# Decode attention started twelve dense units earlier, as one chain of FoX key steps in which VectorE turns K

## What is computed

```python
proj = einsum('bsd,de->bse', h, w_in)                 # q_f k_f v_f f_logit q_d k_d v_d
gates = sigmoid(einsum('bsd,de->bse', h, w_gate) + b_gate)
# FoX, 8 heads, 16 pages of 128 past tokens per sample, taken through page_table
s = einsum('bqhd,bshd->bhqs', q, k) * SCALE + bias_q + bias_k   # bias_k: suffix sum of the cached log forget gates
o_fox = einsum('bhqs,bshd->bqhd', softmax(where(causal, s, NEG)), v)
# dilated windows, 3 groups x 4 heads, keys by stride, T5 bias, merged by their softmax denominators
y = (g_fox * (o_fox @ w_o_fox) + g_dil * (o_dil @ w_o_dil)) @ w_out
```

## Time and profile before

| | us |
|---|---|
| runs, median of 3 | 2433.61 |
| lowest and highest run | 2426.76, 2433.73 |
| the profiled execution | 2423.86 |
| its span | 2422.2 |

### The profile page before, as it was taken

How to read it: one execution, slowest core, us unless ns; L and a number is a source line. 1 busy time by engine, 2 the same in 40 slices (tenths; PEclk the granted TensorE clock), 3 DMA queues, 4 the chain that set the end, 5 groups by cost and what they waited for, 6 DMA issues and landing times.

```text
span 2422.2 us, 45416 instructions
## 1 busy us (share of the span) xinstructions
PE 2330.6 (96%) x18348; PEld 2131.0 (88%) x18348; DVE 1063.4 (44%) x1446; ACT 811.0 (33%) x986; POOL 465.9 (19%) x876
## 2 busy tenths in 40 slices
PE   6999999998999899989989998999999999999998
PEld 6999999998766667666659997999999999999998
DVE  6443434433333333333327437544444444444444
ACT  3233233232433333333412334323333232323334
POOL 2120000002233233323321230311111111111110
PEclk8999999999999999999999999999999999999999
DMA  8474535436899999999976644767677767688894
GB/s 251 141 218 154 155 120 163 152 113 203 279 361 363 340 339 360 362 330 352 343 264 209 217 139 146 267 232 250 228 233 238 245 224 239 222 286 267 288 308 131
DMA packets 337905, 589.57 MB, mean 243 GB/s; under 512 B 17503, under 2 KB 279971, under 8 KB 334079
## 3 DMA queue, kind: packets, MB, share of 16 engines
q0 software_dynamic: 68112, 312.68, 36.7%
q1 hardware_dynamic: 269648, 274.86, 35.8%
HBM read 564.06 MB, written 113.06 MB: 280 GB/s over the span
## 4 chain that ended last, share of the span: by engine, by line
PE 83%; DMA 10%; issue 2%; DVE 2%; ACT 1%; POOL 1%; SPq 0%; POOLq 0%; DVEq 0%; ACTq 0%
PE ps L838 15%; PE ps L839 15%; PE ps L840 15%; PE ps L876 6%; PE ps L878 6%; PE ps L877 6%; DMA kraw<-in_cache_win_k 4%; DMA kraw<-in_cache_fox_k 3%; PE ps L1066 3%; PE ps L1071 2%; PE ps L1091 2%; PE ps L1151 2%; PE ps L1055 2%; PE ps L1057 1%; PE ps L1056 1%
## 5 line engine op out<-in xcount | busy, mean ns | idle before, releaser
L1692 DVE TENSOR_TENSOR w_lo<-raw,w_hi 128x2048 fp32r<-128x2048 f32 (+2 forms) x248 | 526.6, 2124 | 762.3 <-ACT w_hi L1359 762.3
L1359 ACT ACTIVATE w_hi<-raw 128x2048 fp32r<-128x2048 f32 (+2 forms) x248 | 435.6, 1756 | 1032.6 <-PE ps L840 732.6
L838 PE MATMUL ps<-act_hi,w_hi 128*128 128x320 f32 x1616 | 499.6, 309 | 2.0 <-DVE w_lo L1692 2.0
L840 PE MATMUL ps<-act_hi,w_lo 128*128 128x320 f32 x1616 | 499.3, 309 | 0.0
L839 PE MATMUL ps<-act_lo,w_hi 128*128 128x320 f32 x1616 | 499.3, 309 | 0.0
L876 PE MATMUL ps<-act_hi,w_hi 128*128 128x320 f32 x1008 | 318.2, 316 | 0.0
L878 PE MATMUL ps<-act_hi,w_lo 128*128 128x320 f32 x1008 | 312.2, 310 | 0.0
L877 PE MATMUL ps<-act_lo,w_hi 128*128 128x320 f32 x1008 | 312.0, 310 | 0.0
L838 PEld LDWEIGHTS ps<-act_hi,w_hi 128*128 128x128 f32 x1616 | 303.3, 188 | 2.5 <-DVE w_lo L1692 2.5
L839 PEld LDWEIGHTS ps<-act_lo,w_hi 128*128 128x128 f32 x1616 | 303.3, 188 | 0.0
L840 PEld LDWEIGHTS ps<-act_hi,w_lo 128*128 128x128 f32 x1616 | 303.3, 188 | 0.0
(11 more groups left out here) (381 smaller groups left out, 3756.6 us busy)
## 6 DMA issues: line engine op xcount, KB each, us to landing
raw<-in_w_gate_up SPq DMA_DIRECT2D x88, 1024.0 KB, 7.5
kraw<-in_cache_fox_k POOLq DMA_DIRECT2D x128, 512.0 KB, 6.5
vraw<-in_cache_fox_v POOLq DMA_DIRECT2D x128, 512.0 KB, 6.9
raw<-in_w_in SPq DMA_DIRECT2D x60, 1024.0 KB, 7.8
raw<-in_w_down SPq DMA_DIRECT2D x32, 1024.0 KB, 6.0
out_win_k_sample<-in_cache_win_k POOLq DMA_DIRECT2D x64, 510.0 KB, 6.0
out_win_v_sample<-in_cache_win_v POOLq DMA_DIRECT2D x64, 510.0 KB, 4.2
raw<-in_w_gate SPq DMA_DIRECT2D x52, 512.0 KB, 11.0
```

Of the source, the lines that this page charges most:

```text
L838: pe.matmul(ps[:, bk_, 0:T], w_hi[:, slot, k, :], xh[:, x_k, :], start=(k == k0), stop=False)
L840: mm = pe.matmul(ps[:, bk_, 0:T], w_lo[:, slot, k, :], xh[:, x_k, :], start=False, stop=(k == k1 - 1))
L1359: act.activation(w_hi[:, slot, 0:kt, :], raw[:, pslot, 0:kt, P * slot:P * slot + P], ACT.Copy).then_inc(hi_done, 1)
L1692: dve.tensor_tensor(w_lo[:, slot, 0:kt, :], raw[:, pslot, 0:kt, P * half:P * half + P], w_hi[:, slot, 0:kt, :].bitcast(F32), ALU.subtract) ...
```

## The change

- `U_DEC` becomes 52: the last twelve units before the gates' fifth (8 QKV units and 4 gate units) are cut into k blocks and laid between the attention's steps too, with their `take_unit`, `turn` and `nat_rows`. 39 units (52 to 90) are laid over 209 steps instead of 27 over 216.
- The nine sequences become one chain: 128 steps of FoX K blocks, 12 without K, 56 of window K blocks, 13 more. V blocks follow 24 steps behind. `share` sets how many k blocks a step gets: 3 to 4 while FoX V blocks run beside K, 1 or 2 in the window steps.
- FoX K is no longer turned by TensorE. VectorE transposes the block in 32x32 pieces, SBUF to SBUF (`keys_f`), and the queries are spread to a block-diagonal `qb`, so that 32 tiny products (32 columns of weights, 64 moving columns) make the scores of two blocks. The window blocks are still turned by TensorE.
- Because scores now lie on 128 rows (head, part of the block, query), the maximum and the sum over the four parts go through TensorE and back (`turn_top`, `spread_top`, `turn_sum`, `spread_sum`, `fox_top`, ...), and the probabilities are turned by 128 products of 32x32 a sample in place of 16 transposes.
- The bias is written out once and loaded by one DMA of 128 rows of 4 KB a sample. The V ring has 3 slots in place of 4. The prompt's last two dilated heads move into the chain (`head_scores` and on). A panel's four pieces are due two and two, one step apart.

```diff
-        U_DEC = U_GATE + 4
-        STEPS = KPG + 1
-        GATE_UNITS = (4, 3, 3, 3, 4, 3, 3, 3, 1)
+        U_DEC = 52
+        N_FOX, N_DIL, N_WIN = DB * NPG, DB * (KPG - NPG), KPG - NPG
+        V_LAG = NPG + 8
+        K_DIL = N_FOX + 12
+        STEPS = K_DIL + N_DIL + 13
...
+        def share(g):
+
+            if g >= STEPS - 2:
+                return 0
+            if key_block(g) is None or value_block(g) is None:
+                return 16 if g >= V_LAG else 20
+            return 25 if g < V_LAG + N_FOX else 10
...
-            return [U_DEC + m + 2 for m, step_ in enumerate(GATE_DONE) if step_ + (4, 1)[m % 2] + late == STEPS * q + n]
+            return [U_DEC + m + 2 for m, step_ in enumerate(GATE_DONE[:-1]) if step_ + (2, 1)[m % 2] + late == g]
...
-            return min((GATE_DONE[m - 1] if m else -1) + 2 + 2 * j, GATE_DONE[m] + 1)
+            return min((GATE_DONE[m - 1] if m else -1) + 2 + j // 2, GATE_DONE[m] + 1)
...
-        KRING, VRING = 3, 4
+        KRING, VRING = 3, 3
...
+            def keys_f(n):
+
+                dve.wait_ge(k_ld[n % KRING], loads_before(n, KRING))
+                if n % 2 == 0:
+                    wait_pos(dve, sc_done, n // 2)
+                dve.transpose(kS[:, n % 2, :], kraw[:, n % KRING, :]).then_inc(kf_ok, 1)
...
+                for q in range(4):
+                    for e in range(2):
+                        for j in range(4):
+                            c = 32 * (4 * (4 * e + j) + q)
+                            mm = pe.matmul(ps[32 * j:32 * j + 32, 4, 64 * e:64 * e + 64], qb[:, 4 * e + j, q, :],
+                                           kS[:, :, c:c + 32], start=(q == 0 and e == 0), stop=(q == 3 and e == 1), **mmx)
...
+                for k in range(4):
+                    s = 4 * r + k
+                    for e in range(2):
+                        c = 64 * k + 32 * e
+                        for q in range(4):
+                            mm = pe.matmul(ps[32 * q:32 * q + 32, 6 + b % 2 if r % 2 else 5, c:c + 32], fe[e][:, 32 * s:32 * s + 32], selx[:, 32 * q:32 * q + 32],
+                                           start=(k == 0 and e == 0), stop=(k == 3 and e == 1), **mmx)
...
-                for j in range(4):
-                    rows = fbd[2 * j:2 * j + 2, :, b, :].rearrange("h q n -> (h q) n")
-                    pool.dma_start(fb[32 * j:32 * j + 2 * DT, :], rows).then_inc(fb_ld, 16)
+                pool.dma_start(fb[:].rearrange("p e n -> p (e n)"), fbd[b].rearrange("r i n -> (r i) n")).then_inc(fb_ld, 16)
```

957 lines of the change are left out of this document (625 added, 332 removed).

## The result

The changed kernel takes 2509.66 us (median of 4 runs, 2507.48 to 2520.82), the kernel before 2431.72 us in runs beside it (2426.76 to 2433.73). The ratio is 1.034, with a 95% interval of 1.0315 to 1.0367: slower by 78 us, where 90 us less was forecast. It lies outside the range of the prediction.

The account below looks back on a forecast made before the run. TensorE-bound work without DMA stood beside DMA-short decode; overlapping them cut the place from 781.6 to 692 us, -90. From the profiled 2423.86 us that gave 2334, plus 9.75 for the runs' median: 2344 us, range 2300 to 2412.

Parts of the forecast that it names:

- K turned by VectorE: FoX K blocks: 1.3 us each on VectorE, 132 us off TensorE, waits behind K costed at nothing within three steps.
- below any step forecast here: VectorE's work per FoX step, 2.3 us in all, was claimed to be less than any forecast step.
- Weights come late: Rival, chance 0.2: chain weight panels land late beside K and V, +55 us, 2399 us.
- gaps of 3 to 6 us before a unit's first k block: Sign of late weights: TensorE gaps once a panel, released by `w_lo` and behind it the raw load.
- 8.6 steps: Time after which TensorE wants a panel's first unit, 31 us, against 33 us to load plus 2.3 for the halves.
- the objection that stalled time isn't lost to DMA: Argument against late weights: when TensorE stalls, K and V stop and the panel gets the whole DMA rate.
- one even load: Bias: one load replaces four a sequence, which took some 3 us; no wait for it was in the sum.
- Scores and probabilities: TensorE's short products: 1.0 us for a pair's 64 score records, 0.6 us for a quarter of the probabilities.
- short products are dear: Rival, chance 0.1: score and probability products cost up to 2.2 us a group, +62 us, 2406 us.
- The phases: Chain from unit 52 to 91, each step the greater of TensorE and DMA: 692 us in place of 781.6.
- the latency of three loads: 24 steps with K alone: three loads in flight, 6.5 / 3, set 2.3 us a step; 63 us with the start.
- the 382 of one good stretch of 23 us: Full DMA rate in GB/s, from 743 to 766 in the old trace, used for every step of the chain.

Follow-up runs that it names:

- run 12: run 8 with VectorE transposing each of the 128 FoX K blocks twice: 2462.11 us, 70 us more than run 8.
- Run 5b: The changed kernel with an even dense share, an earlier bias load and an even unit's split one step later: 2446.53 us, against 2474.77 without the later split.
- run 5: The changed kernel with each unit's half of the weight panel loaded by itself, as soon as that unit's split has read it: 2436.24 us.
- Runs 7: run 6 with the same two half loads of the bias issued three steps later in GpSimd's order: 2403.91 us.
- run 9: The changed kernel with only the bias loads edited, in two halves at the later places, panels unchanged: 2484.74 us.
- run 2: The changed kernel with GpSimd issuing the bias load three steps earlier: 2490.29 us.
- run 6: run 5 with each sample's bias also loaded in two halves of its columns: 2437.36 us.
- run 8: Runs 7 with the last two prompt heads' bias tables issued one step earlier, the mended version: 2391.91 us, ratio 0.985 to the kernel before.
- run 13: run 8 with only a quarter of the chain's weight bytes loaded: 2363.71 us, 28 us less than run 8.

## Why the prediction was wrong, step by step

**K turned by VectorE: the duration right, the cover wrong.** 1240 ns measured, forecast 1.3 us. The step that failed is the sentence "I cost this at nothing while a block lands within its three steps". It looked at whether VectorE is fast enough and not at what stands ahead of K in its queue. The condition named was the landing of K; what was late was the panel and the bias. One such stall costs K, GpSimd's loads and the scores together, up to 13 us. And without stalls time added to the queue still costs something (run 12). The sum also had VectorE at 2.3 us a step, "below any step forecast here"; the steps with K alone were forecast at 2.3 as well, so there was no room there from the start.

**"Weights come late" was the rival that came true, and was undersized.** It had 0.2 and 2399 us. The cause was the one named, panels that land late, and the time for a panel's load was nearly right (22 us forecast, 17 to 23 in the chain; 86 GB/s for 76). The path was not: the sign was to be gaps of 3 to 6 us before a unit's first k block, and TensorE has only two of these, 12.6 us; it stands before the score products instead, 80 us, since K and the work on the scores before come behind the split in VectorE's queue (a part of the 80 is the late bias). And two numbers were wrong. The time to load was set at 8.6 steps, the pitch of a panel. With one buffer for two units it is from two steps after the odd unit's end to the even unit's split, two steps after that unit's end: one unit, 4.3 steps of 3.75 us, 16 us. Before, it was a unit and two steps, 8 or 10 steps of 3.35 us (80.3 us for 24), 27 to 33 us, and one panel was late. The units became shorter (4.3 steps for 6 or 8) and the split moved from four steps after a unit's end to two; the second stands in the diff, and the sum doesn't mention it. Run 5b gives the price of a single step of it, 28 us. And the objection that stalled time isn't lost to DMA was false: while the panel lands, the K and V blocks already issued still take their four fifths; then they are used up, none has been issued for 13 us, and DMA falls to 112 GB/s. Forecast 4 us a panel and 55 in all; measured 13 us of ScalarE's wait at each of twelve panels, and 73 us given back by run 5. The four pieces were also due closer together than before (`j // 2` for `2 * j`), which no run tests by itself.

**The bias load "one even load", at nothing: 32 us.** The load is even, but it was never placed: GpSimd issues it where VectorE already wants it, and earlier it can't go without holding GpSimd up. Runs 7 and 9 put it at 25 to 32 us; the plain earlier load of run 2 gave 19 of these, and run 6, with the loads where GpSimd has to wait for VectorE, none. The loads of the heads' tables, which the sum didn't mention, gave 12 (run 8). The prediction counted instructions that move, but not at which step of its own engine each stands.

**Scores and probabilities: right.** 64 score records take 0.88 us from first start to last at the full clock (1.08 to 1.10 to the end of the last), forecast 1.0. A quarter of the probabilities takes 0.57 us from first start to last, forecast 0.6. The rival "short products are dear" falls: its 2.2 us appear nowhere, and the groups at 1.62 us run at a granted clock of 0.50 to 0.52. The Trainium skill (TensorEngine Tiling (Array Packing), Instruction Overhead) has some 60 cycles a matmul, by the prediction's estimate 25 ns a record. This trace disagrees: 64 records in 0.88 us are 14 ns each.

**The phases.** What the sum had, what the change took, and what the mended version takes:

| phase | forecast | change | run 8 |
|---|---|---|---|
| 24 steps, K alone | 63 | 88 | 82 |
| 104 steps, K and V | 390 | 517 | 411 |
| 12 steps, V alone | 25 | 32 | 31 |
| 12 steps, window K | 47 | 55 | 50 |
| the rest | 167 | 173 | 172 |
| sum | 692 | 865 | 746 |

The sum as a method stands: with most of the stalls gone its large terms are met within 6% (411 for 390, 172 for 167). The start is the exception: the latency of three loads (2.3 us a step) wasn't the bound there; a step takes 3.4 us, with VectorE busy for 54 of 82 us, TensorE for 63. In the 104 steps DMA is full at 345 GB/s, not at the 382 of one good stretch of 23 us: a window as long as a sequence in the trace of the kernel before has less at a share just as full:

```profile
726.00:806.00 80.00, 75.48 (x844) 54.00 (x844) 29.64 (x66) 30.62 (x55) 28.32 (x54) 1.00 0.99 352
```

This was the row to take. At 345 GB/s the forecast's 1.36 MB a step take 3.95 us, which is what a step of run 8 takes (411 / 104); this shows that the bytes were right, not that DMA alone sets the pace, and run 13 speaks against that. The V ring of 3 slots in place of 4, which the sum doesn't mention, is part of the change too, and no run tests it: in run 8's 104 steps loads of `vraw` make up 10.3% of the chain of waits.

**The clock** isn't in the sum at all. After waits part of the products run at the lower level (the group at 745.81 above); TensorE's busy time in the place is 31 us longer in the change than in run 8. This cost is inside the steps listed below and wasn't separated from them.

From the forecast to the change, as differences of runs that follow each other: 2344 + 48 (run 8 against the forecast) + 12 (heads) + 32 (bias) + 73 (panels) = 2509, the change's 2510 but for rounding. Such a list closes by itself; what supports its terms is that the bias gives much the same alone (25, run 9). The 117 us are shown by edits. The 48 are not divided: the start, the DMA rate, VectorE's loop and the V ring are candidates, and how much each takes stays open.

## What to carry to other kernels

Before you move work onto an idle engine, list what stands ahead of it in that engine's queue and what each of those waits for; its busy share says nothing about it, and a stream that passes through an in-order queue inherits every wait in it. For each load write down when its buffer comes free and when its data are wanted, in the steps of the engine that issues it: a buffer whose two halves are loaded together leaves the time of one unit, a table of distances in steps has to be read again when the step gets shorter, and an engine that runs ahead by a ring must have its other loads placed by that ring. When one load is late, look for an earlier place (halves of the buffer) before you look for more bandwidth.

## What the runs showed of the hardware

- Queues share the DMA engines nearly packet for packet: 862 to 861 with two, 921, 1081 and 917 with three. A queue with rows of 1 KB gets 86 of 388 GB/s beside one with 4 KB.
- VectorE transposes 128 x 1024 fp32 in its 32 x 32 blocks from SBUF to SBUF in 1240 ns, about the time of a subtraction of the same size (1219).
- The granted clock is part of the price of a stall: TensorE's busy time in the place was 689 us at 0.89 and 658 us at 0.96, for the same products. One group of 64 short records takes 0.88 us at a clock of 1.00 and 1.62 us at 0.50 to 0.52.
- A full DMA isn't one number: 388 GB/s over 10 us, 345 over 411 us at a share of 0.98, with rows of 4 KB and 512 bytes mixed.
